# Attention started on seven of nine projected chunks, with two lower halves of the output weights made after it

## The reference, cut to what matters

```
z = h @ w_in                                  # 4608 columns: q_a k_a v_a | q_b k_b v_b | u_c v_c
u_c, v_c = gelu(z[..., 3584:4096]), gelu(z[..., 4096:4608])
o_a, o_b = attention(q_a, k_a, v_a, ...), attention(rope(q_b), rope(k_b), v_b, ...)
o_c = u_c * (w_s @ layer_norm(v_c) + b_s)
x = x + gate * rms_norm(concat(o_a, o_b, o_c) @ w_out)
```

## Time and profile before

| | |
|---|---|
| median of 3 runs | 2321.32 us (2320.76 to 2325.68) |
| the profiled execution's own time | 2317.93 us |
| its span, first to last instruction | 2316.2 us |
| PE busy | 2247.0 us, 97% |
| DVE, ACT, POOL busy | 1622.3, 984.9, 66.5 us |
| moved by DMA | 609.91 MB, 263 GB/s over the span |
| granted TensorE clock, mean | 0.996 |

### The profile page before, as it was taken

How to read it: one execution, slowest core, us unless ns; L and a number is a source line. 1 busy time by engine, 2 the same in 40 slices (tenths; PEclk the granted TensorE clock), 3 DMA queues, 4 the chain that set the end, 5 groups by cost and what they waited for, 6 DMA issues and landing times.

```text
span 2316.2 us, 27842 instructions
## 1 busy us (share of the span) xinstructions
PE 2247.0 (97%) x10614; PEld 1778.0 (77%) x10614; DVE 1622.3 (70%) x1734; ACT 984.9 (43%) x1277; POOL 66.5 (3%) x97
## 2 busy tenths in 40 slices
PE   5999989999999999999999999999999999999998
PEld 3766666678888888888877886787888888888886
DVE  3555473488988989889887996557888544554555
ACT  3333253464444444334446344346444444434443
POOL 1000120000000000000000101000000000000000
PEclk9999999999999999999999999999999999999999
DMA  9899989868878878888866998766887666666664
GB/s 364 323 334 341 337 317 330 300 220 289 282 271 292 289 265 283 295 279 290 307 209 225 312 315 283 271 204 207 270 263 263 185 196 185 190 189 193 191 225 146
DMA packets 269365, 609.91 MB, mean 263 GB/s; under 512 B 19100, under 2 KB 19280, under 8 KB 267824
## 3 DMA queue, kind: packets, MB, share of 16 engines
q1 hardware_dynamic: 264832, 589.37, 75.4%
q0 software_dynamic: 4400, 18.75, 2.3%
HBM read 603.79 MB, written 5.45 MB: 263 GB/s over the span
## 4 chain that ended last, share of the span: by engine, by line
PE 87%; DVE 4%; DMA 4%; ACT 3%; issue 1%; POOL 1%; SPq 1%; POOLq 0%; DVEq 0%; ACTq 0%
PE bank_A L961 41%; PE bank_B L961 39%; DMA mraw<-in_mod_w 3%; PE bank_X L1049 2%; PE bank_M L1025 2%; DVE wlo L1564 1%; PE bank_M L1009 1%; ACT junk L1285 1%; ACT whi L1271 1%; DMA x<-in_x_sample 0%; DVE x L1674 0%; ACT prob L1436 0%; PE bank_M L950 0%; DVE xt_lo L1615 0%; PE bank_T L1042 0%
## 5 line engine op out<-in xcount | busy, mean ns | idle before, releaser
L1564 DVE TENSOR_TENSOR wlo<-raw,whi 128x1024 fp32r<-128x1024 f32 x724 | 880.6, 1223 | 587.3 <-ACT whi L1271 586.4
L1271 ACT CAST whi<-raw 128x1024 fp32r<-128x1024 f32 x724 | 759.5, 1051 | 1162.6 <-PE bank_A L961 575.5
L961 PE MATMUL bank_B<-whi,xt_lo 128*128 128x512 f32 x1104 | 433.3, 392 | 0.0
L961 PE MATMUL bank_A<-whi,xt_lo 128*128 128x512 f32 x1088 | 428.9, 394 | 3.7 <-DVE xt_lo L1615 3.7
L961 PE MATMUL bank_B<-wlo,xt_hi 128*128 128x512 f32 x1104 | 430.0, 389 | 0.0
L961 PE MATMUL bank_B<-whi,xt_hi 128*128 128x512 f32 x1104 | 429.8, 389 | 0.0
L961 PE MATMUL bank_A<-wlo,xt_hi 128*128 128x512 f32 x1088 | 425.0, 391 | 0.0
L961 PE MATMUL bank_A<-whi,xt_hi 128*128 128x512 f32 x1088 | 424.7, 390 | 0.0
L1585 DVE SCALAR_TENSOR_TENSOR acc<-mraw,cond,acc 128x1024 f32<-128x1024 f32 x300 | 371.2, 1279 | 0.0
L961 PEld LDWEIGHTS bank_A<-whi,xt_lo 128*128 128x128 f32 x1088 | 205.0, 188 | 65.1 <-issue 23.2
L961 PEld LDWEIGHTS bank_B<-whi,xt_lo 128*128 128x128 f32 x1104 | 207.2, 188 | 53.8 <-issue 11.7
(11 more groups left out here) (242 smaller groups left out, 1567.7 us busy)
## 6 DMA issues: line engine op xcount, KB each, us to landing
mraw<-in_mod_w SPq DMA_DIRECT2D x352, 512.0 KB, 6.0
raw<-in_w_gate SPq DMA_DIRECT2D x176, 512.0 KB, 4.4
raw<-in_w_up SPq DMA_DIRECT2D x176, 512.0 KB, 4.4
raw<-in_w_down SPq DMA_DIRECT2D x176, 512.0 KB, 5.0
raw<-in_w_in SPq DMA_DIRECT2D x144, 512.0 KB, 5.4
raw<-in_w_out SPq DMA_DIRECT2D x64, 512.0 KB, 5.8
z<-in_mod_w SPq DMA_DIRECT2D x12, 512.0 KB, 11.5
spare<-in_mod_w SPq DMA_DIRECT2D x8, 512.0 KB, 9.5
```

Of the source, the lines that this page charges most:

```text
L961: mm = pe.matmul(bank[f"{pair}{s}"][:], xs[:, k, t], w[:, kb, :], start=(k == first and n == 0), stop=(k == (nk - 1 if last is None else l ...
L1271: act.copy(weights(u * UNIT + ph)[0], raw[:, ph % RING]).then_inc(hi_ready, 1)
L1564: dve.tensor_tensor(lo, raw[:, ph % RING], hi.bitcast(F32), ALU.subtract).then_inc(lo_ready, 1)
```

## The change

A constant `LATER = 2` is added, and:

- the list of steps begins with two turns, then burst 0, then both gelus, and the step ("z",) is gone. PE waits before the list for `z_but_two` (chunks 0 to 6 read), ACT waits for `z_complete` only at its first gelu, GpSimd waits for `z_but_two`, and in layer 1 also until vector 9 has been read out of `turned_b`;
- ACT runs one-element-wide activations (`first_use`) of Gelu ahead of the list, and of Exp ahead of its wait for the first maxima, so that each function's table is loaded there;
- DVE makes the lower halves of pieces 2 and 3 of `w_out` after the attention and no more before the read-out of chunk 8;
- SP loads pieces 6 and 7 of `w_out` after the loads of burst 6 and no more behind those of burst 3. (Their `raw` places are free only when those two lower halves are made.)

```diff
+LATER = 2
 def attention_steps():
-    s = [("burst", 0), ("z",), ("gelu", 0), ("turn", 0, 1), ("turn", 0, 3), ("turn", 0, 0), ("turn", 0, 2), ("turn", 0, 4), ("gelu", 1)]
+    s = [("turn", 0, 1), ("turn", 0, 3), ("burst", 0), ("gelu", 0), ("gelu", 1), ("turn", 0, 0), ("turn", 0, 2), ("turn", 0, 4)]
...
+        first_used = sb("first_used", [P, 2 * DEPTH])
...
+        def z_read(engine, l, last=0):
+            for b in ("A0", "A1", "B0", "B1"):
+                engine.wait_ge(freed[b], plan.at[(l, "att")][2][b] + 1 - last)
+
         def z_complete(engine, l):
-            for b in ("A0", "A1", "B0", "B1"):
-                engine.wait_ge(freed[b], plan.at[(l, "att")][2][b] + 1)
+            z_read(engine, l)
+        def z_but_two(engine, l):
+            z_read(engine, l, 1)
...
@@ SP, attention @@
                     if i == 3:
-                        both(u, w, 0, js=range(LEAD, UNIT))
+                        both(u, w, 0, js=range(LEAD, UNIT - LATER))
+                both(u, w, 0, js=range(UNIT - LATER, UNIT))
                 mi, js = OUT_MODS[l][min(OUT_MODS[l])]
                 mod_chunk(m + mi, l, js)
@@ GpSimd @@
-                z_complete(pool, l)
+                z_but_two(pool, l)
+                if l:
+                    pool.wait_ge(acc_read, MOD_DVE.index(9) + 1)
@@ PE, attention @@
+                z_but_two(pe, l)
...
-                    elif kind == "z":
-                        z_complete(pe, l)
@@ ACT, attention @@
-                z_complete(act, l)
+                first_use(ACT.Gelu_apprx_tanh, 2 * l)
...
                         s = step[1]
+                        if s == 0:
+                            z_complete(act, l)
...
+                        if n == 0:
+                            first_use(ACT.Exp, 2 * l + 1)
                         act.wait_ge(nm_ready, 4 * l + n + 1)
...
+            def first_use(function, i):
+                act.activation(first_used[:, i:i + 1], minus_half[:, 0:1], function)
@@ DVE, start (layer 0) @@
-                    split(0, q + LEAD)
+                    if q < ND * QUARTER - LATER:
+                        split(0, q + LEAD)
@@ DVE, layer 1 and the stage after the attention @@
-                    ahead(split, u + W_INC - 1)
+                    ahead(split, u + W_INC - 1, 0, UNIT - LATER)
                     read_out(u + W_INC - 1, (W_INC - 1) * CH, "A")
                 attention(l)
                 u, m, use = plan.at[(l, "out")]
+                for j in range(LEAD - LATER, LEAD):
+                    split(u, j)
```

## The result

| | before | after |
|---|---|---|
| median of the runs timed side by side | 2322.08 us (9 runs) | 2327.97 us (9 runs, 2325.70 to 2330.22) |
| ratio, with its 95% interval | | 1.0028 [1.0019, 1.0037] |
| profiled execution, its span | 2317.93, 2316.2 us | 2325.77, 2324.0 us |
| granted TensorE clock, mean | 0.996 | 0.993 |

The change makes the kernel 5.9 us slower. I had forecast 2322.6, with a range up to 2326.2.

A forecast was written before the change was run, and what follows sets the result against it. PE, busy 97% of the span, was taken as the bound. Attentions win 0.7 + 1.1 = 1.8 us, output projections lose 0.3 + 2.8 = 3.1: net +1.3 on 2321.3, so 2322.6 us, range 2317.2 to 2326.2.

The forecast's parts named there:

- What is late next: burst 1: Attention: burst 1's later loads make PE wait; of 2.4 us won, 0.7 remain in layer 0, 1.1 in layer 1.
- The stores' start: Layer 1: stores of keys and values start at 1419 to 1421, after rotary work of 7.7 us.
- The amount: Layer 1: 0.2 MB of stores beside burst 1's loads, at 401 GB/s, 0.5 us.
- all stores in front of them: Lower bound of each layer's attention gain, -0.5: 1.05 MB of stores ahead of burst 1's loads, 2.6 us.
- (1): Attention: DVE's read-out of chunk 8 directly behind chunk 7's; score 6.7 us behind the last chunk, in place of 9.1.
- (2): ACT's early Gelu table load takes 1.28 us; with the skill's drain of 1.38 the score would win 1.0, not 2.4.
- (3): Layer 0's attention: PE waits 1.6 us for burst 1's loads, landing after up to 7.4 us; 0.7 us remain won.
- (4): Layer 1's output projection: first burst's loads queue later on SP; loses 2.8 us, wait about 3.5 us in total.
- (5): Layer 0's output projection: the same later loads have slack 2.5 us, so it loses 0.3 us.
- Two remainders of the prediction: The attention gains left after burst 1's wait and the stores: 0.7 us in layer 0, 1.1 in layer 1.
- rival "slow": Output projection's first burst waits for SP's queue in both layers: 2326.3 us at its middle, 2328.6 at most; 13%.
- brings nothing by itself: Attention: early rotary work wins nothing, being done by 306.80 already, with its turns still behind burst 1.

The follow-up runs named there:

- experiment 1: The changed kernel with GpSimd's rotary work and stores waiting for the whole of z again, in both layers: 2323.50 us, ratio to before 1.0004.
- experiment 2: The changed kernel, rotary work early, but the stores of keys and values held to a point behind burst 1: 2322.64 us, ratio to before 1.0001.
- experiment 4: The changed kernel with GpSimd waiting for all of z and the output projection's first-burst loads before `w_out` pieces 6 and 7: 2317.07 us, ratio to before 0.9977.
- Experiment 3: The changed kernel with SP issuing the loads of the output projection's first burst before `w_out` pieces 6 and 7: 2322.73 us, ratio to before 1.0005.
- 10: The changed kernel with stores held behind burst 1, first output burst's loads before `w_out` pieces 6 and 7, burst 0 before the two turns: 2316.58 us, ratio 0.9983.
- experiment 5: The changed kernel with GpSimd waiting for the whole of z again and `LATER = 0`: 2320.35 us, ratio to before 0.9994.
- experiment 9: The changed kernel with rotary work early, only the stores held to behind burst 1, and `LATER = 0`: 2319.39 us, ratio to before 0.9994.
- experiment 7: The changed kernel with rotary work early, stores held to behind burst 1, and first output burst's loads before `w_out` pieces 6 and 7: 2316.94 us, ratio 0.9974.
- experiment 6: The kernel before with only GpSimd's part of the change, rotary work and stores beginning early: 2321.76 us, ratio to before 1.0000.

## Why the prediction was wrong

**The step that failed** is in "What is late next: burst 1": the stores that "run partly beside burst 1's loads: an estimate of 0.2 MB at the 401 GB/s seen under load, 0.5 us. There remain 1.1 in layer 1." With the stores out of the way (experiments 1 and 2) layer 1's attention is at -1.65 and -1.67; with them, at +4.04. The term is 5.7 us, eleven times what I put. Three things in it were off:

- *The stores' start.* I had them at 1419 to 1421. They began at 1424.38, 1.1 us behind the end of the chunk and not 1 to 3 ahead of it, for the start (1414.81) came later than I took, and the rotary work took 9.6 us instead of 7.7. I had carried a duration from a stretch in which DVE makes no lower halves to one in which it does; both took longer there.
- *The amount.* So not 0.2 MB of them but all 1.05 MB were moved before the last load had landed (that was at 1436.2, and GpSimd's queue moved its 1.05 MB between 1420 and 1436). It landed 9.5 us after its issue and not 6.5. This is the bound I had written down ("all stores in front of them", 2.6 us); the waits in burst 1 were 2.18 + 1.55 = 3.73 against 0.65 without the stores, 3.1 us more.
- *The clock.* The rest of the term, 2.6 us, is the stretch at 1.2 GHz behind these waits. It was in none of my bounds. An idle PE was priced at its idle time alone.

**What was right.** (1) The read-out follows that of chunk 7 but for 0.46 us of waiting for PE, and the score comes 6.7 us behind the last product in both layers, as written. (2) Gelu's table load took 1.28 us and the activation followed 0.01 later, so what I took from the row held. The trace does not show the drain that the Trainium skill (ScalarE: Activation LUTs, "What ACT_TABLE_LOAD costs") adds to the load. (3) Layer 0's attention has the wait in burst 1, but its size was off: 0.53 us and not 1.6, so 1.8 won instead of 0.7. Its last load landed 6.2 us after the issue and not 7.4, the one slow landing that I had gone by. The early stores are not the reason: in experiment 4, with late ones, it took 6.1 us. (Two remainders of the prediction are also 0.1 us small: 2.4 - 1.6 is 0.8, and 1.7 - 0.5 is 1.2.) (4) Layer 1's output projection: 2.8 forecast, +2.83 measured, by a wait of 3.4 us in total (3.5 forecast). Experiment 3 shows the cause, SP's order. This agrees with the Trainium skill (DMA: Bandwidth & Descriptors, "Queues, rings and completion order"), by which each DMA engine takes the descriptors of one ring in order. (5) Layer 0's: 0.3 forecast, 0.14 at that burst. Most of the rest of the stage's +1.2 lies in two later bursts, where PE waits 0.32 and 1.27 us in place of one wait of 0.80 before. All other kernels with `LATER = 2` but 10 wait at the second of these places too, by 0.29 to 1.32 us; before and the kernels with `LATER = 0` don't. No run tests why.

With the measured terms, the two attentions and the two first output bursts give -1.82 + 4.04 + 0.14 + 2.83 = +5.2, and the medians differ by 5.9. My rival "slow" had the size of the result, 2326.3 to 2328.6, but by luck: it put the whole price behind the attention.

Two conclusions about the edit itself. `LATER = 2` is needed: without it, in experiments 5 and 9, no attention gains. But it holds back two lower halves on DVE and two raw pieces on SP, and no run separates them. The traces show both at work: without it the score comes 1.1 us or more later than in after, and burst 4 waits 0.57 to 1.39 us for its loads. What the early tables do was not tried alone. The early rotary work "brings nothing by itself", I wrote, and that held: experiments 4 (late) and 7 (early) have -1.93 and -1.94 us in layer 0.

## What to carry over

When a step moves, ask for its duration again at the new place: what runs beside it there, on the engines that slowed it or that it slows. Traffic that moves ahead of a load with no slack is priced by its whole size, and where it makes PE wait for microseconds, a stretch at the lower clock behind the wait belongs into the bounds. Of a bundle of edits, try each alone: here the rest of the bundle won 4.9 us (experiment 4), and two parts of it hid that twice over.

## What was unexpected of the hardware

- GpSimd and DVE instructions that run side by side take longer, on both sides. Four multiplications of 128x256 took 4.79 us instead of 2.77 beside lower halves; a lower half took 2.15, 1.66 and 1.79 instead of 1.23 (experiment 6; after has one of 2.15); the scaling of 128x6 maxima took 1.44 (experiment 1) and 1.49 (5) instead of 0.17, ending as GpSimd's addition ended. The Trainium skill (SBUF — State Buffer, "Who interferes with whom") calls the port pair that both share an exclusive lock, held for a whole instruction by whoever starts first. The short DVE instruction agrees with it. No row here shows which of the two held the ports.
- The lower clock behind a wait is not a matter of the wait's length alone. In layer 1's attention waits of 2.46 + 0.75 us (experiment 3) and of 2.50 (experiment 6) were followed by it (0.51 and 0.52 of 2.4 GHz), waits of 1.62 (experiment 5) and 2.16 (experiment 9) were not. In the first output burst of layer 1 waits of 1.79 + 1.39 us were, for 6.8 us (experiment 2), and longer ones of 2.02 + 1.39 were not (after). In a later burst of layer 0's output projection a wait of 2.50 us was (before), one of 2.78 was not (experiment 7).
